# Spreading the sample's queries with TensorE instead of with DMAs, and loading all eight rows' keys at once

## What is computed

```python
# prompt: banded attention + dilated attention, output projection, then PEER
# sample: the same for 8 single tokens (rows r = 0..7), against caches
kv_a = concat([cache_swa_kv, new_a])     # 128 cached rows, 2 key heads, 8 query heads
kv_b = concat([cache_dil_kv, new_b])     # 1024 cached rows, 8 heads, three dilations
s = einsum('nshgd,nskhd->nshgk', q, kv_g[:, :, :, 0]) * HEAD_DIM ** -0.5
o = einsum('nshgk,nskhd->nshgd', softmax(s), kv_g[:, :, :, 1])
xs = x + concat([rms_norm(o_a), rms_norm(o_b)]) @ w_out
# PEER, for each of the 1032 tokens: 8 heads x 16 experts picked out of 16384
act = gelu(einsum('cd,chkd->chk', h, u[eid]))
x = x + einsum('chk,chkd->cd', gate * act, v[eid])
```

## Time and profile before

| | |
|---|---|
| median of 3 runs | 3265.84 us (3263.42 to 3266.49) |
| the profiled execution | 3275.52 us, of which the span of the trace is 3273.7 us |
| PE, DVE, ACT, POOL busy | 84%, 77%, 56%, 43% of the span |
| moved by DMA | 1262.55 MB, mean 386 GB/s |
| HBM read / written | 1251.24 / 43.37 MB |

### The profile page before, as it was taken

One profiled execution on the slowest core, in us unless ns is written; L12 is line 12 of the kernel. 1 busy time (PEld: TensorE's weight loads), 2 busy tenths in 40 slices (PEclk: granted clock), 3 DMA queues, 4 the chain that ended last, 5 costly groups with the idle time before them and its releaser, 6 DMA issues.

```text
span 3273.7 us, 38234 instructions
## 1 busy us (share of the span) xinstructions
PE 2734.6 (84%) x9152; PEld 1497.6 (46%) x9152; DVE 2532.3 (77%) x6009; ACT 1827.8 (56%) x5820; POOL 1411.1 (43%) x1044
## 2 busy tenths in 40 slices
PE   7777798889989889989988888579878778878886
PEld 4444354445545545554445545234444334444442
DVE  1288687888788998878888887656989987777775
ACT  1245544678555668755556677344555555555554
POOL 0034232444333444434344454223444456666663
PEclk9888999999999999989999999799999999999998
DMA  9999899999999999999999999988999999999997
GB/s 335 357 387 397 338 392 419 385 377 409 399 391 417 388 398 400 387 365 422 390 361 396 383 395 409 351 300 346 373 372 391 386 403 418 421 420 421 416 418 295
DMA packets 191372, 1262.55 MB, mean 386 GB/s; under 512 B 24849, under 2 KB 32873, under 8 KB 46737
## 3 DMA queue, kind: packets, MB, share of 16 engines
q0 software_dynamic: 149760, 1086.39, 82.5%
q1 hardware_dynamic: 41384, 173.70, 14.2%
HBM read 1251.24 MB, written 43.37 MB: 395 GB/s over the span
## 4 chain that ended last, share of the span: by engine, by line
DMA 28%; DVE 26%; PE 24%; issue 7%; ACT 6%; DVEq 5%; POOL 2%; SPq 1%; ACTq 1%; POOLq 0%
DMA uv_ring<-in_peer_uv,idx 25%; DVE uv_ring L2467 10%; PE acc L1775 9%; DVE accs L2474 5%; PE pS L1530 4%; PE pS L1657 3%; PE pA L1680 2%; POOL uv_ring L1471 1%; ACT bent L2072 1%; ACT wv L2075 1%; ACT diag L1845 1%; DVE onehot L2326 1%; DVE onehot L2329 1%; PE acc L1530 1%; PE pS L1584 1%
## 5 line engine op out<-in xcount | busy, mean ns | idle before, releaser
L1471 POOL DMA_INDIRECT uv_ring<-in_peer_uv,idx x1024 | 1394.5, 1362 | 1816.5 <-PE acc L1775 1352.5
L1775 PE MATMUL acc<-uv_ring,diag 128*128 128x512 f32 x2460 | 1242.9, 638 | 378.5 <-ACT diag L1845 373.3
L2467 DVE SCALAR_TENSOR_TENSOR uv_ring<-uv_ring,hb 128x1024 f32<-128x1024 f32 x1032 | 1240.2, 1221 | 280.0 <-DMA uv_ring<-in_peer_uv,idx 253.5
L1775 PEld LDWEIGHTS acc<-uv_ring,diag 128*128 128x128 f32 x2460 | 454.0, 198 | 943.2 <-ACT diag L1845 525.7
L2068 ACT ACTIVATE cube<-dots 128x1 f32<-128x1 f32 x1032 | 205.8, 199 | 874.5 <-DVE uv_ring L2467 866.2
L2474 DVE SCALAR_TENSOR_TENSOR accs<-uv_ring,wv,accs 128x1024 f32<-128x1024 f32 x409 | 523.4, 1280 | 44.0 <-ACT wv L2075 42.1
L1789 PE MATMUL acc<-maskB,zeros 128*96 128x256 f32 x2162 | 520.8, 384 | 0.0
L1789 PEld LDWEIGHTS acc<-maskB,zeros 128*96 128x96 f32 x2162 | 353.4, 165 | 205.5 <-issue 118.1
L2072 ACT ACTIVATE bent<-dots,cube 128x1 f32<-128x1 f32 x1032 | 399.1, 387 | 74.1 <-issue 2.8
L1845 ACT ACTIVATE diag<-diag,wv 128x128 f32<-128x128 f32 x615 | 247.0, 402 | 50.8 <-issue 1.4
L2075 ACT ACTIVATE wv<-bent,dots 128x1 f32<-128x1 f32 x615 | 238.0, 387 | 43.9 <-issue 1.4
(11 more groups left out here) (279 smaller groups left out, 2225.2 us busy)
## 6 DMA issues: line engine op xcount, KB each, us to landing
wbuf<-in_w_q SPq DMA_DIRECT2D x40, 1024.0 KB
out_dil_s<-in_cache_dil SPq DMA_DIRECT2D x8, 4092.0 KB
wbuf<-in_w_in SPq DMA_DIRECT2D x26, 1024.0 KB
wbuf<-in_w_out SPq DMA_DIRECT2D x20, 1024.0 KB
uv_ring<-in_peer_uv,idx POOLq DMA_INDIRECT x1024
uv_ring<-in_w_in SPq DMA_DIRECT2D x6, 1024.0 KB, 16.3
keysT<-in_keys SPq DMA_DIRECT2D x40, 128.0 KB
T<-in_xT_all SPq DMA_DIRECT2D x8, 512.0 KB, 15.1
```

What stands on the lines that cost most here:

```text
L1471: pool.indirect_dma_start(uv_ring[:, entry % RING, :], None, peer_uv, bass.IndirectOffsetOnAxis(rows, 0))\
L1775: m = pe.matmul(acc[0:R, side * 512:(side + 1) * 512], w, uv_ring[:, entry % RING, D + side * 512:D + (side + 1) * 512], start=first, stop ...
L2467: dve.scalar_tensor_tensor(row, row, GELU_C, h, ALU.mult, ALU.mult, accum_out=dots[:, e % RING:e % RING + 1]).then_inc(u_dot, 1)
```

## The change

1. `sample_keys` no longer loads spread queries, has no sets and no wait: all eight rows' keys (`s_kv`, 1024 columns a row in `KTB` and `VB`; near keys in `o_all` and `wbuf`) are asked for at `sin`, four DMAs a row, ahead of the masks.
2. A new stage `sq` for each row, on PE: two matmuls of 512 columns with contraction over 8 partitions. Their weights are column r of an identity, broadcast to 128 columns, and they write the row's query on all 128 partitions of `pS` (even rows) or `pT` (odd rows) in PSUM. `smul` reads it there. `sq` of row r waits for `smul` of row r − 2; `smul` of row r waits for `sq` of row r.
3. The values of row r go where its keys were, and are asked for right after `smul` of row r.
4. The planner's costs and ready times follow: `sq` costs 0.9 us; `sin` and the first two `sq` are ready 10 us later (`NEW_ROWS`); keys of row r are due 6 + 3r us after `sin`, values 14 us after the row's `smul`; `sin` counts as 12 us of other DMA traffic, each `smul` as 1.5.

```diff
 def sample_stages():
     out = [("sin", 0, 0, 0, 0.0, 2.0)]
+    out += [("sq", 0, 0, 1, 0.9, 0.0)]
     for r in range(NS):
-        out += [("smul", r, 0, 2, 0.0, 2.6), ("smul", r, 1, 0, 0.0, 1.6)]
+        out += [("sq", r + 1, 0, 1, 0.9, 0.0)] if r + 1 < NS else []
+        out += [("smul", r, 0, 1, 0.0, 2.6), ("smul", r, 1, 0, 0.0, 1.6)]
...
+    if kind == "sq":
+        return at("smul", a - 2, 1) if a > 1 else last("n3") + last("sm") + last("ng")
+    if kind == "smul":
+        return at("sq", a, 0)
...
-S_SETS = 4
+NEW_ROWS = 10.0
...
-        if s[0] in ("smul", "spv"):
-            return 1.9
+        if s[0] == "sin":
+            return 12.0
+        if s[0] == "smul" and s[2] == 1:
+            return 1.5
...
+        if BASE[n][0] == "sin" or BASE[n][0] == "sq" and BASE[n][1] < 2:
+            ready += NEW_ROWS
...
-            if BASE[n][0] == "spv":
-                m = AT["smul", S_SETS + r // 2, 1]
-            else:
-                m = AT["sin", 0, 0] if r < S_SETS else AT["smul", r - S_SETS, 1]
+            m, late = (AT["smul", r, 1], FETCH + 2.0) if BASE[n][0] == "spv" else (AT["sin", 0, 0], 6.0 + 3.0 * r)
...
-            ready = max(ready, end + FETCH)
+            ready = max(ready, end + late)
...
             def sample_keys(r):
-                i = r % S_SETS
-                if r >= S_SETS:
-                    sp.wait_ge(s_mul, r - S_SETS + 1)
-                for dst, src in cache_rows(s_k[i], r, 0):
-                    sp.dma_start(dst, src).then_inc(sk_in[i], 16)
...
-                sp.dma_start(s_q[i][:, 0:512], zS_scr[r:r + 1, QA:KVA].broadcast_to([P, 512])).then_inc(sk_in[i], 16)
-                sp.dma_start(s_q[i][:, 512:1024], zS_scr[r:r + 1, QB:KB].broadcast_to([P, 512])).then_inc(sk_in[i], 16)
+                for dst, src in cache_rows(s_kv[r], r, 0):
+                    sp.dma_start(dst, src).then_inc(sk_in[r], 16)
...
             def sample_values(r):
-                sp.wait_ge(s_mul, S_SETS + r // 2 + 1)
+                sp.wait_ge(s_mul, r + 1)
...
-                        for r in range(S_SETS):
+                        for r in range(NS):
                             sample_keys(r)
...
-                        if s[1] + S_SETS < NS:
-                            sample_keys(s[1] + S_SETS)
-                        else:
-                            for r in range(2):
-                                sample_values(2 * (s[1] - S_SETS) + r)
+                        sample_values(s[1])
...
+            def sample_queries(r):
+                if r == 0:
+                    pe.wait_ge(snew_in, 64)
+                    need(pe, a_max, seen["sm"])
+                if r == 1:
+                    need(pe, n_T, seen["ng"])
+                if r > 1:
+                    pe.wait_ge(s_mul, r - 1)
+                for side in range(2):
+                    m = pe.matmul(s_q[r % 2][:, 512 * side:512 * side + 512], idn[0:8, r:r + 1].broadcast_to([8, P]),
+                                  s_newq[:, side, :], start=True, stop=True)
+                m.then_inc(sq_mm, 1)
...
             def sample_products(r, part):
                 if part == 0:
-                    dve.wait_ge(sk_in[r % S_SETS], 96 * (r // S_SETS + 1))
+                    dve.wait_ge(sk_in[r], 64)
+                    dve.wait_ge(sq_mm, r + 1)
```

More of the change, by code:

```diff
@@ L292, in times_of @@
         "r0": (("DVE", 3.23),), "r1": (("DVE", 2.75),), "ge": (("ACT", 0.15),),
-        "sin": (("DVE", 2.2),), "smul": (("DVE", 2.62 if b == 0 else 1.55),), "ssc": (("PE", 1.0),),
+        "sin": (("DVE", 2.2),), "smul": (("DVE", 2.62 if b == 0 else 1.55),), "ssc": (("PE", 1.0),), "sq": (("PE", 0.9),),
         "ssm": (("DVE", 2.6),), "sse": (("ACT", 1.2),), "ssd": (("DVE", 1.16),), "spr": (("PE", 0.6),),
@@ L1045, in build @@
         VBf = VB[:, :, :].rearrange("p t n -> p (t n)")
[L1046 to L1050, removed]
+        s_kv = [(KTBf if r < 4 else VBf)[:, 1024 * (r % 4):1024 * (r % 4) + 1024].rearrange("p (s n) -> p s n", s=2)
+                for r in range(NS)]
         s_prod = rest[:, 0:1024]
@@ L1059, in build @@
         s_newA = o_all[0:8, 0:256]
-        s_kA = [o_all[:, 256 + P * i:384 + P * i] for i in range(S_SETS)]
+        s_kA = [o_all[:, 256 + P * r:384 + P * r] if r < 6 else rest[:, 2752 + P * (r - 6):2880 + P * (r - 6)]
+                for r in range(NS)]
         s_vA = [S[:, P * r:P * (r + 1)] for r in range(NS)]
@@ L1078, in build @@
         pA = pb("pA", [P, 512])
+        s_q = [pS, pT]
         c_in = sem("c_in")
@@ L1096, in build @@
         smask_in = sem("smask_in")
-        sk_in = [sem(f"sk_in{i}") for i in range(S_SETS)]
+        sk_in = [sem(f"sk_in{r}") for r in range(NS)]
+        sq_mm = sem("sq_mm")
         sv_in = [sem(f"sv_in{r}") for r in range(NS)]
@@ L1324, in sample_keys @@
             def sample_keys(r):
-                i = r % S_SETS
-                if r >= S_SETS:
-                    sp.wait_ge(s_mul, r - S_SETS + 1)
-                for dst, src in cache_rows(s_k[i], r, 0):
-                    sp.dma_start(dst, src).then_inc(sk_in[i], 16)
-                sp.dma_start(s_kA[i], cache_swa[r:r + 1, :].rearrange("r (s n) -> (r s) n", n=256)[:, 0:P])\
-                  .then_inc(sk_in[i], 16)
-                sp.dma_start(s_q[i][:, 0:512], zS_scr[r:r + 1, QA:KVA].broadcast_to([P, 512])).then_inc(sk_in[i], 16)
-                sp.dma_start(s_q[i][:, 512:1024], zS_scr[r:r + 1, QB:KB].broadcast_to([P, 512])).then_inc(sk_in[i], 16)
+                for dst, src in cache_rows(s_kv[r], r, 0):
+                    sp.dma_start(dst, src).then_inc(sk_in[r], 16)
+                sp.dma_start(s_kA[r], cache_swa[r:r + 1, :].rearrange("r (s n) -> (r s) n", n=256)[:, 0:P])\
+                  .then_inc(sk_in[r], 16)
             def sample_scores_out():
@@ L1359, in sample_values @@
             def sample_values(r):
-                sp.wait_ge(s_mul, S_SETS + r // 2 + 1)
+                sp.wait_ge(s_mul, r + 1)
                 if r == 0:
                     sp.wait_ge(n_t, NT)
-                for dst, src in cache_rows(s_v[r], r, 1):
+                for dst, src in cache_rows(s_kv[r], r, 1):
                     sp.dma_start(dst, src).then_inc(sv_in[r], 16)
@@ L1747, in sample_pv @@
                 pe.wait_ge(sv_in[r], 64)
-                pe.matmul(pS[0:64, 0:512], s_pT[:, 0, c], s_v[r][:, 0, :], start=False, stop=False)
-                pe.matmul(pS[0:64, 0:512], s_pT[:, 1, c], s_v[r][:, 1, :], start=False, stop=last)
+                pe.matmul(pS[0:64, 0:512], s_pT[:, 0, c], s_kv[r][:, 0, :], start=False, stop=False)
+                pe.matmul(pS[0:64, 0:512], s_pT[:, 1, c], s_kv[r][:, 1, :], start=False, stop=last)
                 pe.matmul(pS[0:64, 512:640], s_pT[:, 2, c], s_vA[r], start=False, stop=last).then_inc(s_pv, 1)
@@ L1826, in _ @@
                     key_scores(s[1], s[2])
+                elif kind == "sq":
+                    sample_queries(s[1])
                 elif kind == "ssc":
@@ L2409, in sample_products @@
                 if part == 0:
-                    dve.wait_ge(sk_in[r % S_SETS], 96 * (r // S_SETS + 1))
-                    dot_heads(s_sc[:, 0:2, 8 * r:8 * r + 8], s_k[r % S_SETS].unsqueeze(2),
-                              s_q[r % S_SETS][:, 512:1024].unsqueeze(1).unsqueeze(1).broadcast_to([P, 2, 1, 512]),
+                    dve.wait_ge(sk_in[r], 64)
+                    dve.wait_ge(sq_mm, r + 1)
+                    dot_heads(s_sc[:, 0:2, 8 * r:8 * r + 8], s_kv[r].unsqueeze(2),
+                              s_q[r % 2][:, 512:1024].unsqueeze(1).unsqueeze(1).broadcast_to([P, 2, 1, 512]),
                               1024, P, (2, 1, 2))
                 else:
-                    dot_heads(s_sc[:, 2:3, 8 * r:8 * r + 8], s_kA[r % S_SETS].rearrange("p (a d) -> p a d", a=2)
+                    dot_heads(s_sc[:, 2:3, 8 * r:8 * r + 8], s_kA[r].rearrange("p (a d) -> p a d", a=2)
                               .unsqueeze(2).broadcast_to([P, 2, 4, HD]),
-                              s_q[r % S_SETS][:, 0:512].rearrange("p (b a d) -> p a b d", a=2, b=4), 512, P, (2, 4, 1))\
+                              s_q[r % 2][:, 0:512].rearrange("p (b a d) -> p a b d", a=2, b=4), 512, P, (2, 4, 1))\
                         .then_inc(s_mul, 1)
```

## The result

The changed kernel takes 3239.62 us (median of 5 runs, 3228.76 to 3251.01) against 3266.49 for the kernel before in the same comparison. The ratio is 0.9904, 95% interval 0.9875 to 0.9933: 27 us by the medians, 31 by the ratio, 22 to 41 by the interval. The forecast was 17 us and 3249, with a range of 3233 to 3270. So direction and range held, and the size was larger than forecast. The profiled execution took 3239.62 us, 36 less than that of before, which at 3275.52 us lies above the median of its own runs. So the two traces show more than the runs do.

What follows compares the result with a forecast made beforehand. The prediction took the DMA engines, full from end to end, as the bound. Its terms, −14 − 5 + 2 = −17 us, took the profiled 3275.5 to 3258.5, divided by 1.0030 to 3249 us; range 3233 to 3270.

Steps and rivals of the forecast that it cites:

- What bounds the kernel: Whole kernel: the 16 DMA engines are busy end to end, so a byte not moved is time saved at the end.
- The removed transfers: Sample's attention: dropping 16 query-spread transfers of 256 KB, 4.19 MB, gains 14 us (10 to 16).
- the price of SP's queue: Sample's attention, 2040 to 2160: SP's transfers cost 3.60 us per MB, so the removed bytes are worth 15.1 us.
- that of a gather's bytes: Low end for the removed bytes: they cost no more than gather bytes, 2.38 us per MB, so 10.0 us.
- Keys at once: Sample's attention: the burst of keys costs nothing; values land earlier, cutting waits of PE and DVE, 5 us gained (0 to 9).
- the mark of being right: Sign of success: no stretch before the output projection with a DMA share under 0.9.
- The added matmuls: PE in the sample's attention: `sq` takes about 1.9 us per row, mostly covered, 2 us lost (0 to 5).
- rival d: Sample's attention: PE and DVE wait for each other, 24 us of idle DMA, +10 us net, or 3276; chance 0.1.
- The order planned anew: Planner's new order in the last group: counted only as a risk that eats the gain, with an 11 us loss.
- its own 12 us of idle DMA: Output projection on PE, 2200 to 2260: DMA share 0.80, 12 us idle, which the change doesn't touch.
- rival c: Last group: changed planner costs shift the order and lose 11 us, leaving −6, or 3260, at worst 3266; chance 0.15.
- Rival (a): Sample's attention and output projection: the stage recovers more, including 8 of the projection's 12 us; −33, or 3233; chance 0.15.

Runs made afterwards that it cites:

- The part alone in the old order: Kernel before with queries spread by 16 PE matmuls into PSUM instead of 16 DMAs, every other instruction keeping its place: 0.9966, 11 us faster.
- The run with late values: Changed kernel with values asked for in pairs after `smul` of rows 4 to 7, instead of one row after each `smul`: 0.9919.

## Why the prediction was right in direction and short in size

**What bounds the kernel: right.** The gain stays from gather 820 to the end, 35.5 and 35.9 us. What is won in the stage, less the transfers that only moved behind it, arrives at the end.

**The removed transfers, 14 us (10 to 16): right size, in one setting.** The part alone in the old order gave 11 (6 to 17), with the 2 us for the matmuls in it, so 13 by the forecast's own split. It can't tell 10 from 14, so it doesn't decide between the price of SP's queue in the earlier trace rows and that of a gather's bytes. But it isn't a fixed price: with keys at once and room for two spread queries the same transfers cost 21 us, and there the trace shows them as a stall too. The prediction counted bytes alone and nothing for the 16.6 us that DVE waited; 11 us with the four sets leave little room for these waits, so most of them seem to have been covered.

**Keys at once: right that they cost nothing, wrong in how.** I expected the values to have long landed. They hadn't. SP in the changed kernel, first and last issue of dilated keys, then the first and the last of the values; start, us it took, instruction:

```profile
2051.19 1.29 SPq L1333 DMA_DIRECT2D KTB<-in_cache_dil  x3
...
2098.50 3.00 SPq L1333 DMA_DIRECT2D VB<-in_cache_dil  x3
...
2104.16 1.48 SPq L1366 DMA_DIRECT2D KTB<-in_cache_dil  x3
...
2143.19 1.33 SPq L1367 DMA_DIRECT2D S<-in_cache_swa  x1
```

SP needed 50 us to issue the keys, because from row 3 on single issues of three transfers took up to 10 us. The values of row 0 were asked for at 2104, 25 us after its `smul`, which ended at 2079. The run with late values issued them at nearly the same times, which fits that the two can't be told apart.

The prediction's reading of before has the same gap: it laid the late last values to their room, which came free at 2142. SP's last issue of three before that transfer started at 2151 and took over 10 us by itself:

```profile
2151.25 10.49 SPq L1364 DMA_DIRECT2D VB<-in_cache_dil  x3
```

The 20 us from 2142 to 2161.79 were SP's issuing and not a wait for room. The waits of the changed kernel in 2040 to 2200:

```profile
DVE wbuf L2463 <- PE pS L1762: 13.4, 1, 13.4
...
DVE wbuf L2403 <- DMA o_all<-in_cache_swa: 10.5, 3, 6.3
...
PE pS L1760 <- DMA S<-in_cache_swa: 8.4, 2, 6.5
```

`smul` still waited 10.5 us, now for keys, and PE 8.4 us for the last values (6.5 before), with DVE standing 13.4 behind them (22.3 before). The run of `smul` went from 2072 to 2132, 60 us instead of 80. It started later, as `sin` did (new queries asked for at 2050.86 instead of 2040.64); counted from there it ended 20 us earlier, inside the 15 to 30 that I expected, and by the clock of the trace 10. Of the 5 us that I gave to this step the trace has about 3: a share of 0.84 instead of 0.77 in the 40 us from 2160 to 2200. No run shows that early values or keys at once brought them, and 0.84 is under the 0.9 that I had named as the mark of being right.

**The added matmuls: right.** The trace has them at the length taken from the fold, twice the planner's figure:

```profile
2063.60 1.98 PE L1729 MATMUL pS<-qT,idn 8*128 8x512 f32 x4
...
2103.03 3.78 PE L1729 MATMUL pT<-qT,idn 8*128 8x512 f32 x4 [6.48 <-DVE PT L2405]
```

Seven of the eight took 1.9 to 2.0 us, one 3.78. Reading the query out of PSUM cost nothing: `smul` takes 1.22 us as before. Mutual waiting of PE and DVE (rival d) is there in one row, the 6.48 us above (DVE itself stood for keys), with 1.4 and 0.7 us in two more, and the share of the whole stretch 2040 to 2160 stayed at 1.03.

**The order planned anew: this is the term that failed.** The prediction wrote that the projection "keeps its own 12 us of idle DMA", and counted the new plan only as a risk, a loss of up to 11 us (rival c). It was the largest single gain. With the old allowance the change is worth 15 us (11 to 20), near the 17 of the forecast, and the allowance adds 16. That the 15 lie so near is in part luck: that run too has the later `sin` and the new ready times, and the 5 us for keys and values in the forecast's sum are not shown by any run. The row was there to be read: PE busy for 60.00 of 60 us at a DMA share of 0.80 doesn't mean that PE can't feed the ring, it means that the order gives it too few places; with 24 us of allowance the kernel before starts 18 gathers instead of 16 in the same PE work. The diff lowered the allowance from 24 x 1.9 = 46 us to 12 + 8 x 1.5 = 24 while the transfers fell only from 13.6 to 9.4 MB, and I read it as bookkeeping that follows the change. Rival (a) named the right place and the right 8 to 12 us of idle, but laid it to freer engines and not to the order.

## What to carry to other kernels

When a kernel's order comes out of a planner, treat each changed cost of the planner as an edit of its own and price it where it makes the plan denser or thinner; a planner that sets aside more time for transfers than it must weaves too little into its busiest engine, and that engine's busy time doesn't show it (54.64 us both ways), only the DMA share and the count of gathers. Before crediting an edit, run the new order with the old operations: here that split 31 us into about 20 and 11. A broadcast by DMA costs most where other transfers are queued ahead of it: the same 4.2 MB cost 11 us in one arrangement and 21 in the other, where the query of row 2 stood behind 32 key transfers.

## What the runs showed of the hardware that I had not expected

SP's issues can stretch: three transfers that take 1.3 us to issue took 8 to 10 us each during the burst of keys, and all that SP had to issue afterwards waited for them. It isn't the burst alone, for the kernel before has such issues too (8.96 us at 2091.38, 10.49 at 2151.25). They come after several transfers asked for in close succession; what holds them up isn't shown. And in the kernel before the DMA engines stayed full (share 1.04 in 2040 to 2160) while DVE and PE both stood still for up to 10 us at a time, since the sample's own transfers took 38% of them beside the gathers' 65%. The idle time came only behind that stage, 0.77 and 0.80 in 2160 to 2260.
